# Decode attention over a paged cache: block transposes on VectorE, 32x32 array tiles, page loads issued by SP and POOL

## The reference

```python
past_ckv = cache_ckv[page_table].reshape(B, -1, KV_LORA)      # B = 8, 4096 tokens, 256
past_kr = cache_krope[page_table].reshape(B, -1, QK_ROPE)     # 32
q_lat = jnp.einsum('blhd,chd->blhc', q_nope, w_uk)            # 8 heads
s_past = (jnp.einsum('blhc,btc->bhlt', q_lat, past_ckv)
          + jnp.einsum('blhr,btr->bhlt', q_rope, past_kr)).astype(jnp.float32) * ATTN_SCALE
s_new = ...                                                   # the same against the new token
p = jax.nn.softmax(jnp.concatenate([s_past, s_new], axis=-1), axis=-1)
o_lat = (jnp.einsum('bhlt,btc->blhc', p[..., :T], past_ckv)
         + jnp.einsum('bhls,bsc->blhc', p[..., T:], ckv))
return jnp.einsum('blhc,chd->blhd', o_lat, w_uv)
```

## Time and profile before

| | |
|---|---|
| median of 3 runs | 1611.43 us (1607.24 to 1612.15) |
| profiled execution | 1615.35 us |
| its span | 1613.4 us, 24089 instructions |
| TensorE busy | 1383.7 us (86%), weight loads 1118.7 us (69%) |
| VectorE busy | 950.3 us (59%) |
| ScalarE busy | 663.6 us (41%) |
| GpSimd busy | 175.5 us (11%) |
| mean granted TensorE clock | 0.922 of full speed |

### The profile page before, as it was taken

How to read it: one execution, slowest core, us unless ns; L and a number is a source line. 1 busy time by engine, 2 the same in 40 slices (tenths; PEclk the granted TensorE clock), 3 DMA queues, 4 the chain that set the end, 5 groups by cost and what they waited for, 6 DMA issues and landing times. The chain is left out here.

```text
span 1613.4 us, 24089 instructions
## 1 busy us (share of the span) xinstructions
PE 1383.7 (86%) x8142; PEld 1118.7 (69%) x8142; DVE 950.3 (59%) x1422; ACT 663.6 (41%) x902; POOL 175.5 (11%) x254
## 2 busy tenths in 40 slices
PE   4989999896788888777679993799999999936997
PEld 4989999785454465555458872688888888825886
DVE  4457566653677633333244445688888888745653
ACT  5222344320566522212132111677777777633221
POOL 6000211051000010000001000000000000012310
PEclk9999999796899989989879995899999999967999
DMA  5121211475984046555272220469656999935410
GB/s 182 31 78 40 69 53 54 159 224 160 322 305 112 1 127 182 164 169 169 65 240 104 105 92 26 171 245 357 247 219 217 333 404 405 378 141 206 157 66 39
DMA packets 131791, 275.02 MB, mean 170 GB/s; under 512 B 23601, under 2 KB 58930, under 8 KB 131378
## 3 DMA queue, kind: packets, MB, share of 16 engines
q1 hardware_dynamic: 116706, 217.16, 40.4%
q0 software_dynamic: 11824, 45.11, 7.7%
q10 hardware_dynamic: 3168, 11.54, 1.8%
HBM read 214.34 MB, written 58.38 MB: 169 GB/s over the span
## 5 line engine op out<-in xcount | busy, mean ns | idle before, releaser
L399 PE MATMUL pb<-xH,wH 128*128 128x344 f32 x432 | 142.5, 330 | 26.4 <-DVE wL L858 10.9
L400 PE MATMUL pb<-xL,wH 128*128 128x344 f32 x432 | 140.1, 324 | 0.0
L401 PE MATMUL pb<-xH,wL 128*128 128x344 f32 x432 | 140.0, 324 | 0.0
L2507 DVE TENSOR_TENSOR downL<-raw_down,downH 128x2048 fp32r<-128x2048 f32 x44 | 98.9, 2288 | 44.5 <-ACT downH L2409 39.4
L2409 ACT CAST gateH<-raw_gate 128x2048 fp32r<-128x2048 f32 x44 | 83.8, 1910 | 66.8 <-PE pb L2342 40.8
L2507 DVE TENSOR_TENSOR gateL<-raw_gate,gateH 128x2048 fp32r<-128x2048 f32 x44 | 100.5, 2287 | 15.8 <-ACT gateH L2409 15.8
L399 PEld LDWEIGHTS pb<-xH,wH 128*128 128x128 f32 x432 | 83.0, 192 | 28.9 <-issue 10.8
L2507 DVE TENSOR_TENSOR upL<-raw_up,upH 128x2048 fp32r<-128x2048 f32 x44 | 100.3, 2282 | 1.0 <-ACT upH L2409 1.0
L1477 PE MATMUL pb<-cst,pages 128*128 128x128 f32 x512 | 73.7, 309 | 28.7 <-DMA pages<-in_cache 27.2
L1477 PEld LDWEIGHTS pb<-cst,pages 128*128 128x128 f32 x512 | 66.8, 160 | 37.0 <-DMA pages<-in_cache 32.0
L1646 DVE COPY pgT<-pb 128x512 f32<-128x512 f32 x64 | 41.9, 687 | 79.4 <-PE pb L1477 78.9
(11 more groups left out here) (447 smaller groups left out, 3279.1 us busy)
## 6 DMA issues: line engine op xcount, KB each, us to landing
pages<-in_cache SPq DMA_DIRECT2D x256, 144.0 KB, 2.4
raw_gate<-in_w_gate SPq DMA_DIRECT2D x32, 1024.0 KB
raw_up<-in_w_up SPq DMA_DIRECT2D x32, 1024.0 KB, 8.2
raw_down<-in_w_down SPq DMA_DIRECT2D x32, 1024.0 KB, 8.5
y_d<-yzero POOLq DMA_DIRECT2D x4, 4096.0 KB, 31.0
y_d<-yo ACTq DMA_DIRECT2D x22, 512.0 KB, 3.9
wraw_p<-in_w_blk SPq DMA_DIRECT2D x18, 512.0 KB, 3.5
xa<-in_x_all SPq DMA_DIRECT2D x9, 512.0 KB, 3.7
```

What stands on the lines that cost most here:

```text
L399: pe.matmul(out, wh, xh, start=first, stop=False)
L400: pe.matmul(out, wh, xl, start=False, stop=False)
L401: return pe.matmul(out, wl, xh, start=False, stop=last)
L2507: dve.tensor_tensor(part(low_[w], c), part(raw[w], c), part(high[w], c).bitcast(F32), ALU.subtract).then_inc(S(w + "_low"), 1)
```

## The change

- **Loads.** The three buffers become a ring of 11 groups of eight pages (`RING3`). For groups 4 to 31, SP issues the first four pages of a group and POOL the other four; each engine reads its own page numbers. From group 11 on both wait until the sequence that used the slot has been weighed. Two semaphores count a group, one per engine. `w_uv` goes where `pgT` lies, so it is loaded after the scores of the last sequence.
- **Transposes.** VectorE transposes eight pages at once in 32x32 blocks, from SBUF to SBUF, rotary values included (`dve.transpose`, 128x2304). There is a single `pgT` of 32 pages; its next use waits for the scores of the sequence before (`past_mm`). TensorE's page transposes, the copies out of PSUM, `krg`, `krT`, `zq` and `zr` go.
- **Scores.** All four groups of a sequence are scored together: for each of nine blocks of 32 values and each of 4 row and 4 column tiles, one matmul of 8 query columns over 256 columns, into four PSUM banks, one per row tile. The query is laid out once, at the start (64 small matmuls, one matmul that repeats it on all partitions, two copies).
- **Softmax and weighing.** The maximum and the exponential run over 1024 columns. The probabilities are turned by eight matmuls against a selection of the identity. ScalarE copies them out, and does the bias copy and the scaled copy of the result. The row sums are two matmuls.
- **Order.** On PE: scores of b, turned probabilities of b-1, maximum of b, half of the weighing of b-1, the bias of b, the other half. The fold over tiles is done once for all sequences, after the last.

The diff, cut to its core:

```diff
@@ loads @@
+        GRPS = 4 * NB
+        RING3 = 11
+        SHARE = {'sp': (0, 4), 'pool': (4, 4)}
+        def load_pages(eng, name, at, first, some):
+            found = nc.values_load_multi_w_load_instructions(
+                pt_sb[0:1, bass.ds(8 * at + first, some)], engines=(ENGINE[name],), min_val=0, max_val=cache.shape[0] - 1)[1]
+            for m, page in enumerate(found):
+                eng.dma_start(group_pages(at)[:, first + m, :], cache[bass.ds(page, 1), :, :].rearrange("a p w -> (a p) w")).then_inc(page_sw[at % RING3] if name == "pool" else page_in[at % RING3], 16)
+        def load_share(eng, name, at):
+            if at >= RING3:
+                eng.wait_ge(S("spv_mm"), (at - RING3) // 4 + 1)
+            load_pages(eng, name, at, *SHARE[name])
@@ block.sync @@
-            for b in range(1, NB):
-                if b >= 3:
-                    sp.wait_ge(S("spv_mm"), b - 2)
-                load_pages(sp, b, b % 3)
+            for at in range(4, GRPS):
+                load_share(sp, "sp", at)
+            sp.wait_ge(S("past_mm"), NB)
+            sp.dma_start(wuv, w_uv.rearrange("(c p) n -> p c n", p=P)).then_inc(S("uv_in"), 16)
@@ block.tensor @@
+            for j in range(NJ - 1):
                 for h in range(H):
+                    last = pe.matmul(pb[0:32, 6, (j * H + h) * NB:(j * H + h + 1) * NB], ukt[:, h, 32 * j:32 * j + 32], qd[:, h, :], start=True, stop=True)
+            def scores(b):
+                if b:
+                    pe.wait_ge(S("sexp_rdy"), 2 * b)
+                pe.wait_ge(S("pgT_rdy"), 4 * b + 4)
+                for j in range(NJ):
+                    for r in range(4):
+                        for g in range(4):
+                            at = slice(32 * r, 32 * r + 32)
+                            last = pe.matmul(pb[32 * g:32 * g + H, r, 0:256], q4[at, b, j, :], pgT[at, 8 * g:8 * g + 8, 32 * j:32 * j + 32],
+                                             start=j == 0, stop=j == NJ - 1, skip_group_check=True, tile_position=(32 * r, 32 * g))
+                last.then_inc(S("past_mm"), 1)
...
+            def turn_probs(b):
+                pe.wait_ge(S("sexp_rdy"), 2 * b + 2)
...
+                for x in range(8):
+                    last = pe.matmul(pb[:, 4, 32 * x:32 * x + 32], pexp[:, x, :, :].rearrange("p g t -> p (g t)"), heads, start=True, stop=True)
...
+            scores(0)
+            pe.wait_ge(S("small_zero"), 5)
+            largest_row(0)
+            bound_column(0)
+            for b in range(1, NB + 1):
+                if b < NB:
+                    scores(b)
+                turn_probs(b - 1)
+                if b < NB:
+                    largest_row(b)
+                weigh(b - 1, range(0, PAGES // 2))
+                if b < NB:
+                    bound_column(b)
+                weigh(b - 1, range(PAGES // 2, PAGES))
@@ block.gpsimd @@
+            for at in range(4, GRPS):
+                load_share(pool, "pool", at)
@@ block.vector @@
+            def turn_pages(b, g):
+                pages_in(dve, 4 * b + g)
                 if b:
+                    dve.wait_ge(S("past_mm"), b)
+                dve.transpose(pgT[:, 8 * g:8 * g + 8, :], group_pages(4 * b + g)).then_inc(S("pgT_rdy"), 1)
...
+            dve.memset(pb[:, 0:4, :], 0.0).then_inc(S("b_zero"), 1)
+            dve.memset(pb[:, 7, :], 0.0).then_inc(S("b_zero"), 1)
...
+            for g in range(4):
+                turn_pages(0, g)
+            for b in range(NB):
+                largest(b)
+                if b + 1 < NB:
+                    turn_pages(b + 1, 0)
                 if b:
+                    row_sums(b - 1)
                 row_bounds(b)
+                for g in range(1, 4 if b + 1 < NB else 1):
+                    turn_pages(b + 1, g)
+            row_sums(NB - 1)
```

More of the change, by code:

```diff
@@ L1405, in program @@
         p2a.close()
-        end_phase("dec_in", *[f"page_in0_{g}" for g in range(4)])
+        end_phase("dec_in", *[f"page_in{g}" for g in range(4)])
         p3 = ExitStack()
[L1413 to L1426, removed]
+        pages.append(sb_in(p3, "pages1", [P, 8 * (RING3 - 4), CACHE_W]))
+        page_in.extend([S(f"page_in{n}") for n in range(4, RING3)])
+        page_sw = [S(f"page_sw{n}") for n in range(RING3)]
+        NJ = CACHE_W // 32
+        pgT = sb_in(p3, "pgT", [P, PAGES, CACHE_W])
+        q4 = sb_in(p3, "q4", [P, NB, NJ, H])
+        qlat = sb_in(p3, "qlat", [32, (NJ - 1) * H * NB])
+        four = sb_in(p3, "four", [32, 4, 32])
+        newT = sb_in(p3, "newT", [P, NJ, 32])
+        same = sb_in(p3, "same", [P, 4, 32])
+        snew_s = sb_in(p3, "snew_s", [H, 32])
+        smx = sb_in(p3, "smx", [P, 1])
+        mrow = sb_in(p3, "mrow", [1, 4, 32])
         colmx = sb_in(p3, "colmx", [H, 1])
@@ L1461, in _ @@
[L1461 to L1523, removed]
+            pe.wait_ge(S("qlat_rdy"), 1)
@@ new lines, in _ @@
+            pe.wait_ge(S("small_zero"), 5)
+            pe.matmul(pb[:, 5, :], four[:, :, :].rearrange("p c r -> p (c r)"), qlat[:, :], start=True, stop=True).then_inc(S("q4_mm"), 1)
+            def scores(b):
[9 more added lines that the diff above has]
+                last.then_inc(S("past_mm"), 1)
+                for j in range(NJ):
+                    last = pe.matmul(pb[0:H, 0, 256:288], q4[0:32, b, j, :], newT[0:32, j, :], start=j == 0, stop=j == NJ - 1,
+                                     skip_group_check=True, tile_position=(0, 0))
+                last.then_inc(S("ss_mm"), 1)
@@ L1552, in latent @@
-            def latent(b):
-                pe.wait_ge(S("o_rdy"), b + 1)
-                for c in range(2):
-                    last = pe.matmul(pb[:, 7, 2 * KL - 64 + c * H:2 * KL - 64 + (c + 1) * H], o_sb[:, c * P:(c + 1) * P], sel32, start=True, stop=True,
-                                     skip_group_check=True)
-                last.then_inc(S("olat_mm"), 1)
-            scores(0, 0)
-            for b in range(NB):
-                bounds(b)
-                if b + 1 < NB:
-                    scores(b + 1, (b + 1) % 2)
-                weigh(b, b % 2)
-                latent(b)
@@ L1595, in _, with exps @@
         @block.scalar
         def _(act):
[L1597 to L1604 removed]
+            def exps(b):
+                act.wait_ge(S("nb_mm"), b + 1)
@@ new lines, in _ @@
+            act.wait_ge(S("qlat_mm"), 1)
+            act.copy(qlat[:, :], pb[0:32, 6, :]).then_inc(S("qlat_rdy"), 1)
+            act.wait_ge(S("q4_mm"), 1)
+            act.copy(q4[:, :, 0:NJ - 1, :], pb[:, 5, :].rearrange("p (j h b) -> p b j h", j=NJ - 1, h=H)).then_inc(S("q4_rdy"), 1)
+            act.wait_ge(S("small_zero"), 5)
+            exps(0)
+            for b in range(1, NB + 1):
+                turned_probs(b - 1)
+                if b < NB:
+                    exps(b)
+                latent_out(b - 1)
```

242 lines of the change are left out of this document (94 added, 148 removed).

## The result

The changed kernel takes 1629.61 us (median of 7 runs, 1621.41 to 1633.76), the one before 1611.43 in the same comparison: ratio 1.011, 95% interval 1.0086 to 1.0133. It is 18 us slower, where 15 us less was forecast. The profiled execution spans 1632.1 us against 1613.4.

A forecast was written before the change was run, and what follows sets the result against it. SP's issue of page loads was taken as the bound. Start and sequence 1 to 612.3 us, six periods of 25.5 to 765.3, a 20 us tail to 785.3: 15.1 us saved, 1596 us forecast, range 1556 to 1650.

The forecast's parts named there:

- L: Time from a freed slot to its eight pages landed, issued by SP and POOL: 7.6 us.
- (d): Rival: POOL's page issue becomes the bound; 1691 us at the slowest issue, 1611 if milder; chance 0.09.
- (e): Rival: page loads keep the old pace, so the change buys nothing; 1613 us; chance 0.04.
- T: One block transpose of eight pages on VectorE: 2.55 us.
- (a): Rival: VectorE's fp32 transpose takes two passes, 5.1 us each; kernel 1647 us; chance 0.14.
- Start: Block's beginning: four transposes end at 585.35 us, query layout hidden behind them; scores of sequence 0 end at 592.0.
- S: Scores of one sequence on TensorE, 288 records: 6.6 us.
- (b): Rival: row tiles of the score matmuls do not overlap, scores take 15.4 us; kernel 1667 us; chance 0.07.
- (c): Rival: issue of score records is the limit at 29 ns, scores take 8.4 us; kernel 1611 us; chance 0.11.
- W: From the end of a sequence's scores to the end of the weighing: 8.6 us.
- The loop: Period per sequence, with the last page group waiting for the weighing to free its slot: 25.5 us against 28.0.
- Sum: Block ends at 785.3 us instead of 800.4, 15.1 us saved: kernel 1596 us.

The follow-up runs named there:

- the run with few pages: The changed kernel, but from group 11 on only two of a group's eight pages are loaded, all other instructions kept: 1589.7 us (one run).

## Why the prediction was wrong

- **What bounds the kernel before: right.** SP's issue did. With two issuers the old algorithm runs 1.7% faster.
- **Issue, landing, L: right.** POOL's page took 0.54 us on its engine where 0.60 was taken; L 7.55 for 7.6. Part of that is luck: from the freed slot to POOL's first issue it took 1.95 us (1.75 forecast), between two issues 0.61 (0.78), from the last issue to the transpose 3.78 (3.5), and the errors cancel. Rivals (d) and (e) fell.
- **Transposes, T: right.** 2.56 us for 2.55. (a) fell.
- **Start: 4 us late.** Scores began at 586.2 (585.35 forecast); S of sequence 0 was 10.8. Sequence 1's followed 19.35 later for 20.3. Together 616.3 for 612.3.
- **Scores, S: the mis-sized term**, 9.61 for 6.6 in the loop. The engine's own part was near: low-clock records took 32.3 ns for 27, others 19.0 for 18, and S without its waits is 7.1. (b) fell. (c) was partly right at the low clock (30 ns) and wrong at the full one. The step's 4.1 us of low clock came out (4.2), by luck: it was read from the earlier trace rows as following idle times of 10 us, but TensorE had idled 4.9 us before the first of these stretches and at most 1.5 before the others. The other 2.5 us are instruction packets that came late. The row for them was there, the instruction queue in the DMA view with 15 packets in the block; the step multiplied the records per sequence and never asked what brings them.
- **W, the second mis-sized term**, 10.94 for 8.6. At the full clock it is 7.6, a microsecond better than forecast. 0.6 is two late packets between scores and turning (1.5 and 2.0 us, over six periods). The remaining 2.7 is the low clock, mostly behind breaks: the step took TensorE as warm through turning and weighing, and named the clock's dips only at the start of scores. In the run with few pages four of six periods had none, the two with a break of 1.1 us or more had.
- **The loop: right in form.** 9.61 + 10.94 + 7.55 + 2.75 = 30.85 for a measured 30.8; the same sum holds in the runs with other terms. What it left out is that its terms aren't independent: the weighing frees the slots, so the page bursts begin there and lie on the next scores.
- **Sum.** Six periods of 5.3 too much are 32 us, the start 4, the tail 2 (block end 823.2 for 785.3). 4 us came back in parts that the change doesn't touch: 1 in the block behind, 3 at the last gathers of the kernel; why, no run shows. 32 + 4 + 2 - 4 = 34, the distance from -15 to +19 in the profiled span.

So the change joins a part worth 28 us in the kernel before with a form of scores that loses more. The time lies inside the range, but no rival of the prediction brought it there: late instructions were in none of them.

What stays open: the trace doesn't show when TensorE asks for a packet, so the start behind the load 128 places earlier is a measure, not the wait itself. How far the clock's low stretches in W depend on a break's length was not separated.

## What to carry to other kernels

Count the instructions per microsecond that a new tiling asks of an engine, beside its columns, and look at what else uses the DMA engines then: 288 records of a 32-row tile ran in 7 us without a break where the engines were quiet and the clock low at first, and waited 2.5 us on average in the loop, nearly all of it under bursts of pages. A block-diagonal operand of 128 rows does the same work with a quarter of the records and was 44 us better. And when a loop closes through a buffer, free the buffer in parts and write the loop as a sum; each measured term then shows which step failed.

## What the runs showed of the hardware

- TensorE broke off for 0.85 to 3.55 us at places 128 weight loads (256 instructions) apart when page loads kept the DMA engines 66 to 97% busy, and once for 1.20 us at a share of 0.03. At 72 records in 6 us it didn't, at a DMA share of 1.00.
- TensorE went on 1.20 to 1.63 us after a 16384-byte instruction packet had landed, at 57 breaks in six runs. A packet took 0.88 to 1.74 us. In the changed kernel it started 1.5 to 3.6 us after the load 128 places earlier where page data held 0.71 or more of the DMA engines, and 0.2 and 1.1 us after it at the two places where they held none.
- Records of 32x32 tiles at 16 places of the array: 19.0 ns each at the full clock, 32.3 at half. With half the columns a record took 29.7 at half, so fewer columns gained almost nothing there. The clock stayed at 0.50 through 17 us of such records without a break.
- After breaks in the scores the granted clock over the next 9 to 11 us was 0.68 and 0.81 in the windows shown; without one it was 1.00 twice and 0.81 once.
- VectorE's block transpose of 128x2304 fp32 takes 2.56 us on average of 32, the pace of its other fp32 work.
